# Attention in two layers: the reciprocal of the sums placed behind the next maximum, the short steps' sums taken on VectorE, and TensorE's step begun with the transposes

## The reference, cut to what matters

```python
def masked_softmax(s, mask):
    s = jnp.where(mask, s.astype(jnp.float32), -jnp.inf)
    m = jnp.max(s, axis=-1, keepdims=True)
    m = jnp.where(jnp.isfinite(m), m, 0.0)
    p = jnp.exp(s - m)
    return p / jnp.maximum(jnp.sum(p, axis=-1, keepdims=True), 1e-30)
...
# layer 0, each head: selected keys
s = jnp.einsum('bthd,btkd->bthk', qi, k_sel) * HEAD_DIM ** -0.5
p = masked_softmax(s, valid[:, :, None, :]).astype(v.dtype)
return jnp.einsum('bthk,btkd->bthd', p, v_sel)
...
# layer 1, each head: three branches (31 compressed blocks, selected blocks, window), gated
o = gi[..., 0:1] * o_c + gi[..., 1:2] * o_s + gi[..., 2:3] * o_w
...
# both layers: memory heads over 256 memory rows
p = jax.nn.softmax(s, axis=-1).astype(v.dtype)
return jnp.einsum('bhsn,bnhd->bshd', p, v)
```

## Time and profile before

| | |
|---|---|
| median of three runs | 3491.35 us (3488.41 to 3496.68) |
| the profiled execution | 3488.59 us |
| its span | 3486.4 us |
| mean granted clock of TensorE over the span | 0.966 |
| busy share of the span | TensorE matmuls 94%, weight loads 77%, GpSimd 46%, VectorE 45%, ScalarE 42% |
| attention of layer 0 | 206.90 to 288.98 us |
| attention of layer 1 | 845.97 to 1019.55 us |

### The profile page before, as it was taken

The page is one execution under the profiler, slowest core; times in us unless marked ns, Lnnn a source line. Parts: engine busy times, 40 slices in busy tenths (PEclk is TensorE's granted clock), DMA queues, the critical chain, the costliest instruction groups (busy, mean ns, idle before and its releaser), DMA issues.

```text
span 3486.4 us, 45570 instructions
## 1 busy us (share of the span) xinstructions
PE 3274.7 (94%) x16902; PEld 2672.1 (77%) x16902; DVE 1581.4 (45%) x2319; ACT 1449.8 (42%) x2659; POOL 1598.0 (46%) x1404
## 2 busy tenths in 40 slices
PE   5789999998899999999989896999999999999998
PEld 4467888876568888788878775788888888888886
DVE  4773443142543441344237785565555662234421
ACT  3355333323764333333234554445554542243322
POOL 4245445653455446544552221444444435454454
PEclk8999999997999999999999997999999999999999
DMA  4111333341003333333332211111111113333332
GB/s 118 48 43 55 96 96 94 95 116 37 1 19 97 96 95 94 95 96 96 94 82 61 55 49 31 36 37 37 37 43 38 37 49 97 97 97 96 96 95 68
DMA packets 471306, 245.85 MB, mean 71 GB/s; under 512 B 13820, under 2 KB 468711, under 8 KB 471015
## 3 DMA queue, kind: packets, MB, share of 16 engines
q1 hardware_dynamic: 470144, 241.33, 24.5%
q10 hardware_dynamic: 998, 2.30, 0.2%
HBM read 241.51 MB, written 2.10 MB: 70 GB/s over the span
## 4 chain that ended last, share of the span: by engine, by line
PE 82%; DVE 9%; ACT 4%; issue 3%; POOL 1%; DMA 0%; ACTq 0%; DVEq 0%; POOLq 0%
PE ps L464 18%; PE ps L466 18%; PE ps L465 18%; PE ps L2304 2%; PE ps L2200 2%; PE ps L2202 2%; PE ps L2201 2%; PE ps L2286 2%; PE ps L1534 1%; PE ps L1719 1%; PE ps L1720 1%; PE ps L1721 1%; PE ps L1792 1%; ACT arena L1627 1%; PE ps L1544 1%
## 5 line engine op out<-in xcount | busy, mean ns | idle before, releaser
L446 POOL TENSOR_TENSOR w_lo<-ring,w_hi 128x512 fp32r<-128x512 f32 (+1 forms) x908 | 1222.4, 1367 | 1544.7 <-ACT w_hi L437 1544.7
L437 ACT ACTIVATE w_hi<-ring 128x512 fp32r<-128x512 f32 (+1 forms) x908 | 516.1, 617 | 1276.5 <-PE ps L466 1191.8
L464 PE MATMUL ps<-h_hi,w_hi 128*128 128x512 f32 x1776 | 702.7, 396 | 5.2 <-POOL w_lo L446 4.4
L466 PE MATMUL ps<-h_hi,w_lo 128*128 128x512 f32 x1776 | 693.1, 390 | 0.0
L465 PE MATMUL ps<-h_lo,w_hi 128*128 128x512 f32 x1640 | 640.0, 390 | 0.0
L464 PEld LDWEIGHTS ps<-h_hi,w_hi 128*128 128x128 f32 x1776 | 334.4, 188 | 81.9 <-POOL w_lo L446 6.4
L466 PEld LDWEIGHTS ps<-h_hi,w_lo 128*128 128x128 f32 x1776 | 334.3, 188 | 70.0
L465 PEld LDWEIGHTS ps<-h_lo,w_hi 128*128 128x128 f32 x1640 | 308.9, 188 | 68.5 <-issue 4.8
L465 PE MATMUL ps<-a_lo,w_hi 128*128 128x512 f32 x752 | 292.7, 389 | 0.0
L466 PE MATMUL ps<-a_hi,w_lo 128*128 128x512 f32 x720 | 280.2, 389 | 0.0
L464 PE MATMUL ps<-a_hi,w_hi 128*128 128x512 f32 x720 | 280.2, 389 | 0.0
(11 more groups left out here) (445 smaller groups left out, 5818.0 us busy)
## 6 DMA issues: line engine op xcount, KB each, us to landing
ring<-in_ffn_w_in SPq DMA_DIRECT2D x176, 512.0 KB, 3.8
ring<-in_w_in SPq DMA_DIRECT2D x96, 512.0 KB, 4.0
ring<-in_ffn_w_down SPq DMA_DIRECT2D x32, 512.0 KB, 4.0
ring<-in_ffn_w_out SPq DMA_DIRECT2D x32, 512.0 KB, 3.9
ring<-in_w_o SPq DMA_DIRECT2D x16, 512.0 KB, 4.1
ring<-in_w_branch_gdn SPq DMA_DIRECT2D x16, 512.0 KB, 3.8
ring<-in_nsa_w_in SPq DMA_DIRECT2D x15, 512.0 KB, 3.8
ring<-in_dsa_w_in SPq DMA_DIRECT2D x13, 512.0 KB, 4.0
```

What stands on the lines that cost most here:

```text
L437: act.activation(w_hi[:, (halves(u) + j) % PIECES, 0:n, :], slot(u)[:, j * n:(j + 1) * n, :], ACT.Copy) \
L446: pool.tensor_tensor(w_lo[:, q % PIECES, 0:n, :], slot(u)[:, j * n:(j + 1) * n, :], w_hi[:, q % PIECES, 0:n, :].bitcast(f32), ALU.subtract ...
L464: pe.matmul(dst, wh, hi(k), start=first and k == 0, stop=False)
L466: ins = pe.matmul(dst, wl, hi(k), start=False, stop=last and k == 2 * n - 1)
```

## The change

On TensorE the transposes of step i-3 are issued ahead of the scores of step i; the values of step i-4 stay last. On VectorE the reciprocal of step i-1 is issued behind the maximum of step i. A new function `sum_apart` picks the steps with at most 128 keys (6 in layer 0, 36 in layer 1, 24 of these with 31 keys): their exponentials gather no sum, and VectorE sums the exponentials out of `p_buf` ahead of the reciprocal.

```diff
+    def sum_apart(u):
+
+        return u["nk"] <= P
+
...
     def pe_attention(pe, t, layer):
...
         for i in range(S + LAG_V):
-            if i < S:
-                if i >= 2:
-                    pe.wait_ge(sig("att_prob").sem, t["prob"] + i - 1)
-                for hh in range(2):
-                    u, rows_ = us[2 * i + hh], even_odd[hh]
-                    ins = pe.matmul(ps[:, score_banks(i), 0:u["nk"]][:, hh, :], u["q"][rows_], u["k"][rows_],
-                                    start=True, stop=True)
-                ins.then_inc(sig("att_scores").sem, 1)
             s = i - LAG_T
             if 0 <= s < S:
                 pe.wait_ge(sig("att_norm").sem, t["norm"] + s + 1)
...
                 ins.then_inc(sig("att_turned").sem, 1)
+            if i < S:
+                if i >= 2:
+                    pe.wait_ge(sig("att_prob").sem, t["prob"] + i - 1)
+                for hh in range(2):
+                    u, rows_ = us[2 * i + hh], even_odd[hh]
+                    ins = pe.matmul(ps[:, score_banks(i), 0:u["nk"]][:, hh, :], u["q"][rows_], u["k"][rows_],
+                                    start=True, stop=True)
+                ins.then_inc(sig("att_scores").sem, 1)
             s = i - LAG_V
...
     def dve_attention(dve, ch, t):
...
-            if 1 <= i <= S:
-                before = slice(2 * ((i - 1) % DEEP), 2 * ((i - 1) % DEEP) + 2)
-                dve.wait_ge(sig("att_prob").sem, t["prob"] + i)
-                if us[2 * i - 2]["clamp"]:
-                    ch.link(dve.tensor_scalar(row_sum[:, before], row_sum[:, before], 1e-30, None, ALU.max))
-                dve.reciprocal(row_inv[:, before], row_sum[:, before]).then_inc(sig("att_inv").sem, 1)
             if i < S:
...
                     dve.tensor_reduce(neg_max[:, columns], s, AX, ALU.max, negate=True).then_inc(sig("att_max").sem, 1)
+            if 1 <= i <= S:
+                u, before = us[2 * i - 2], slice(2 * ((i - 1) % DEEP), 2 * ((i - 1) % DEEP) + 2)
+                dve.wait_ge(sig("att_prob").sem, t["prob"] + i)
+                if sum_apart(u):
+                    ch.link(dve.tensor_reduce(row_sum[:, before], p_buf[:, p_slot(i - 1), 0:u["nk"]], AX, ALU.add))
+                if u["clamp"]:
+                    ch.link(dve.tensor_scalar(row_sum[:, before], row_sum[:, before], 1e-30, None, ALU.max))
+                dve.reciprocal(row_inv[:, before], row_sum[:, before]).then_inc(sig("att_inv").sem, 1)
...
     def act_attention(act, t, layer):
...
-                    ins = act.activation(x, ps[:, score_banks(i), 0:nk][:, hh, :], ACT.Exp, bias=neg_max[:, column], accum_out=row_sum[:, column])
+                    ins = act.activation(x, ps[:, score_banks(i), 0:nk][:, hh, :], ACT.Exp, bias=neg_max[:, column],
+                                         accum_out=None if sum_apart(us[2 * i]) else row_sum[:, column])
```

## The result

The change takes **3528.88 us** (median of four runs, 3524.48 to 3531.31) against 3490.84 for the kernel before (four runs beside it). The ratio is 1.0104, interval 1.0083 to 1.0125: slower by 1%. The forecast was 3506, its range ended at 3522. The sign was right, the size was not.

What follows compares the result with a forecast made beforehand. The prediction took a loop through several engines, none full, to set the attention stages' pace. It summed 3488.6 + 6.6 (layer 0) + 4.9 (layer 1) + 6 (clock) = 3506 us, range 3494 to 3522.

Steps and rivals of the forecast that it cites:

- TensorE's order, +6.6 in layer 0: Layer 0: scores behind transposes put a copy into the loop; rounds 11.0 instead of 9.9, six rounds, +6.6 us.
- the two places: Layer 0: the scores of 256 and of 512 keys, which the walk had held up behind copies and transposes.
- Layer 1, +4.9: Layer 1: copy and transposes add to the loop, the freed maximum gives back; rounds 25.7 from 24.91, +4.9 us.
- rival B: Both stages: transposes ready in time, scores lose nothing, only the freed maximum counts; faster, 3477 us, chance 0.07.
- The sum apart, 0: 42 steps: 8 us less on ScalarE, at most 17 more on VectorE, beside other work; costed at nothing.
- rival D: GpSimd holds VectorE's new reduction, or the clock falls in most rounds; 3520 to 3530 us, chance 0.08.
- The memory pairs: 16 steps without a mask: freed maximum and later scores about cancel; 0, between -1 and +1 us.
- three drops more, +6: Attention stages: longer TensorE waits bring three more drops to the lower clock, +6 us, bounds 0 and +20.
- The 2.0 us: Price of one clock drop, from two layer 1 rounds with the same instructions: 26.89 us against 24.91.
- ten of the twelve rounds: Upper bound of the clock term over both stages: drops in ten of the twelve rounds, +20 us.
- more than six rounds with a clock below 1.00: Sign that would show the forecast's clock term wrong, counted over the rounds of the stages.
- The signs of the right loop: Full-clock rounds 11.0 and 25.7; scores waiting for copies or transposes; second 512-key maximum right behind its mask; 84 fewer accumulator reads.

Runs made afterwards that it cites:

- e1: The change's TensorE order alone, with VectorE's order and the sums of the kernel before; 3544.01 us, ratio 1.0143 to the kernel before.
- e5: The change with extra repeated products of the values on TensorE, at steps after which it waits; 3499.10 us, ratio 1.0021 to the kernel before.
- e7: The change with about half as many repeated products on TensorE as e5; 3495.22 us, ratio 1.0001 to the kernel before.
- e4: The change with TensorE's old order, keeping the late reciprocal and the sum apart; 3473.29 us, ratio 0.9944 to the kernel before.
- e2: The kernel before with only the reciprocal moved behind the next maximum; 3476.00 us, ratio 0.9955 to the kernel before.
- e6: The change with TensorE's old order, and new reduction, limit and reciprocal all ahead of the maximum; 3504.04 us, ratio 1.0023 to the kernel before.

## Why the prediction was right and wrong

- **TensorE's order, +6.6 in layer 0: right in place, a little small (7.7).** A full-clock round was 10.85 in e1 and at most 11.19 in e5 and e7, walked 11.0; with the two places put back 10.41, walked 10.35. The wait is for the copy, and in layer 0 the scores waited for exponentials only once in the stage.
- **Layer 1, +4.9: right in kind, a little small (6.4).** A round at the full clock was at most 25.97, walked 25.7. The loss and the gain in it were both there, and their separate sizes are now measured for layer 1: the order on top of the rest costs 2.6 us in a round (25.97 in e7 against 23.33 in e4), and the late reciprocal under the old order is worth 1.6 us in a round (24.91 to 23.3), close to the 11 us in the stage that rival B had counted from the earlier trace rows. B failed only in its condition: the order's cost did not go away.
- **The sum apart, 0: right**, as far as it can be told (e4 against e2, 2.7 us apart). Its reductions took 207 and 408 ns. The first half of rival D, that GpSimd holds them, did not come: in the change they hardly met its work, and in e6, where they did, they kept their time.
- **The memory pairs and the rest.** Layer 0's memory steps took 22.5 us in both kernels. 2.5 us of the span's 41.9 lie outside the stages; the forecast had nothing there.
- **The clock, "three drops more, +6": wrong, and this is the step that failed.** It cost some 25 us above what the kernel before paid, and 30.2 us against e7. The second half of rival D, "the clock falls in most rounds", is what came, and both halves together had 0.08. What was off is chiefly the number of drops. The 2.0 us had come from a round with 6.8 us at the lower clock, 0.29 for each microsecond there. In the change the same division gives 0.37 in layer 0 (13.67 less 11.19, over 6.8) and 0.34 and 0.42 in layer 1 (4.6 over 13.7, 1.4 over 3.4): a little more. But the time at the lower level rose by 71 us in the stages, every round had some, and three rounds of layer 1 had twice that of the priced drop and the first 24. So even the upper bound, "ten of the twelve rounds" with one drop each, +20, was too low, and a range that held it (3520) with 2 us to spare was too narrow.
- With 25.2 in its place (39.3 less 7.7 and 6.4) the sum is 3488.6 + 6.6 + 4.9 + 25.2 = 3525.3. The profiled execution took 3530.07: the two loops came 2.6 longer than walked, and 2.5 lie outside the stages, which leaves less than half a microsecond.
- **Why the number was off.** I took the earlier trace rows, two stretches that looked alike with a drop behind one of them, to say that drops come by chance, and so added a few. They show only that one drop came there and none a round later, and nothing of what longer waits do. The change's waits repeat in each round, and so do its drops: 6.8 us in three successive rounds of layer 0, nearly the same number each time.
- **Of the signs that I had named as wrong**, "more than six rounds with a clock below 1.00" was the one that came, with a small changed time outside the stages. The signs of the right loop came too: scores behind copies and transposes, the second 512-key maximum right behind its mask, 84 accumulator reads fewer. The full-clock rounds of 11.0 and 25.7 could be seen only in e5 and e7, for the change had none.

## What to carry to other kernels

Where a change makes TensorE wait a little longer in every round, allow for the lower clock in every round and price it as a term of its own (here 0.3 to 0.4 us for each microsecond at the lower level), not as a few chance drops; filling the waits with repeats tells it apart from the loop. On an engine that works in program order, as TensorE's program does here, work that waits for a copy should not stand ahead of the work through which the loop runs, and a reciprocal that nobody needs soon should stand behind the maximum that everybody waits for.

## What the runs showed of the hardware that was not expected

- More work made the program faster: e7 has 264 TensorE instructions more than the change in the two stages (681 and 1449 against 585 and 1281), and its ratio is 1.0001 instead of 1.0104.
- In the change TensorE's waits for the copy were 1.8 us at most in layer 0 and 1.4 in layer 1, and every round had a drop; one of the drops set in 1.18 us after the engine fell idle. Waits of 1.26 us at the same place, with a few more products ahead of them (e7), and of 1.30 in the rounds of the kernel before, went by at the full clock.
- The same work at nearly the same pace can go either way: e1 has a round of layer 0 with 8.68 of 10.85 us busy at the full clock, and the rounds behind it have drops. What exactly decides stays open.
- VectorE's reduction ran at its full speed beside GpSimd while the 128x2 operation right behind it took three times its time (e6).
